# Seven small edits around the rotary keys, the query copies, the first loads and the fillers of a two-block transformer kernel

## The chip, the cores and the metric

The kernel runs on one core of one Trainium2 chip. The metric is the device time of one execution in microseconds; the median of three runs stands for a kernel.

## The reference, cut to what matters

Two transformer blocks are applied one after the other to 512 positions of width 1024. The change touches the input projection and the rotary keys of the first block, the norms after its mixing and after its embedding gate, and the final norm. Of the first block:

```python
u = _rmsnorm(h, g_mix_pre[i])
z = u @ w_in[i]                      # conv 3*512, q_lat 384, kv_lat 256, k_pe 32, gates 2*1024
...
q = (_rmsnorm(q_lat, g_q_lat[i]) @ w_q_up[i]).reshape(bsz, s, N_HEADS, QK_DIM)
kv = (_rmsnorm(kv_lat, g_kv_lat[i]) @ w_kv_up[i])
k_pe = _rope(k_pe[:, :, None, :], positions)      # 32 rotary columns, shared by 8 heads
ob = _chunk_causal_attention(q_full, k_full, v)
...
h = h + _rmsnorm(mixed @ w_o[i], g_mix_post[i])
...
return rmsnorm(h, final_norm)                     # end of the second block
```

The second block reads a memory of 256 positions (`mem`), whose keys and values are also projected.

## The kernel before

**Layout.** Activations lie feature-major: a tile is 128 features by 512 positions. `h` holds the residual stream in 8 tiles. All large products run as three matmuls each (`three`): both operands are split into a high part (type fp32r) and a low part, and high x high, low x high and high x low are added in one PSUM bank of `acc`, which is used as a ring of 4 banks. A tile number `t` uses bank `t % 4`; `open_tile(t)` waits until the tile four before it was taken (`acc_free`, counted in order of tiles by DVE).

**Weights.** They come in units of 128 x 1024 (8 blocks of 128 columns), 333 of them before, in the order in which they are used. SyncE's queue loads unit j into one of 2 raw buffers when the unit two before it has been split (`w_split`); GpSimd (POOL) makes the high and the low part (`split`), in a ring of 4; TensorE (PE) waits for `w_split` at each unit. The first unit is split in two parts (`split_first`: 384 and 640 columns).

**Orders written by hand.** Each engine has one program in order, and they meet by semaphores.

- PE: 12 fillers (`idle`) on a zeroed tile; `spread` (the first three conv tiles side by side, k by k, one k needing one tile of the scaled input); `stationary` and `stationary_loop` (one output tile after another). The order of the input projection is: 12 conv tiles (0 to 11), two small tiles of the distance table (L1243), five latent tiles, one tile of 128 columns with the 32 rotary keys and their turned copy, 16 gate tiles. Then 6 query tiles, 4 value tiles (`moving`), 4 key tiles, 7 tiles of `w_a_out` over the conv output `yhi`, and attention. `memory(layer, sums, roots)` projects the memory over 8 steps k, with the sums of squares of the tile just made (`sum_features`) ahead of step `sums` and their roots spread over the partitions (`spread_roots`) ahead of step `roots`. At the end `again(9)` and `again(2)` stand around the last sums.
- DVE: takes tiles from `acc`; for conv tile group i it takes three tiles, applies the three-tap filter, and writes the low part in `conv_low(i)` after ScalarE (ACT) has written the high part. `conv_low(3)` is the end of the conv part. `times_gain` multiplies a narrow weight by a norm's gain; before the change it is used for `wn` and `wn2`, each followed by `wn_ready`. While it takes key tiles (two of the four), it waits for ACT's copies of the other two (`q_copied`) before it frees their banks.
- ACT: after the gates' sigmoids it waits for `kpe_ready`, copies the rotary keys into the 8 heads of `kf` (8 activations, each waited for), copies four query tiles by `pair`, issues 16 DMAs that place the rotated query halves, and copies two key tiles by `pair`.

`narrow(o, w, width, done)` multiplies a narrow fp32 weight with the raw `h`: k's 8 products go to 128/width strips of output partitions, so with width 32 four of them lie side by side and each strip holds a partial sum.

## Time and profile before

| | |
|---|---|
| median of 3 runs | 2060.71 us (2060.5 to 2061.94) |
| profiled execution, own time | 2061.25 us |
| its span in the trace | 2059.4 us |
| PE busy | 2043.0 us |
| PE weight load busy | 1666.7 us |
| POOL busy | 1274.4 us |
| DVE busy | 974.1 us |
| ACT busy | 576.1 us |

Times in the trace count from the start of the span; L12 is line 12 of the kernel. A PE matmul's duration includes its way through the array, so consecutive matmuls overlap: those of 512 columns start about 0.227 us apart when nothing holds them up, and 24 of them (one output tile over 8 k) take 5.44 us. In a row, "x8" is the number of instructions merged in it, and the bracket gives the idle time of the engine just before it and what ended it.

### The profile page before, as it was taken

To read this page: it belongs to the slowest core of one execution; us is meant where nothing else is said; L and a number is where in the kernel's file an instruction comes from. 1 tells how busy PE (TensorE), PEld (TensorE's weight loads), DVE (VectorE), ACT (ScalarE), POOL (GpSimd) and SP (SyncE) were. 2 spreads that over 40 slices of the span, in tenths; PEclk is the share of its full clock that TensorE was granted. 3 is DMA by queue.
4 is the path that set the end of the run, shared out by engine and by line. 5 is a ranking of instruction groups with operands and counts; after the bars stand their busy time and mean duration, and the time that the engine had idled before them with its cause. 6 is when DMAs were issued, how large, how long until landed. Compare 5 with 4: busy or idle time off the path is not lost.

```text
span 2059.4 us, 29727 instructions
## 1 busy us (share of the span) xinstructions
PE 2043.0 (99%) x10041; PEld 1666.7 (81%) x10041; DVE 974.1 (47%) x1719; ACT 576.1 (28%) x1145; POOL 1274.4 (62%) x846
## 2 busy tenths in 40 slices
PE   9999999999999999999999999999999999999998
PEld 7888768788888887899888888888875588888887
DVE  5452464655552055566455555234367535555311
ACT  3211433422220054323342222000247632222100
POOL 7666638866667668432666666666555566666663
PEclk9999999999999999999999999999999999999999
DMA  5323473323233342221123333334410032332332
GB/s 190 92 92 94 112 106 118 107 92 101 93 107 108 102 148 92 73 62 42 62 92 94 100 93 100 102 106 144 144 42 1 12 102 92 93 101 92 102 107 76
DMA packets 56259, 195.09 MB, mean 95 GB/s; under 512 B 6355, under 2 KB 6803, under 8 KB 55924
## 3 DMA queue, kind: packets, MB, share of 16 engines
q1 hardware_dynamic: 49824, 178.30, 27.7%
q10 hardware_dynamic: 6356, 15.72, 3.4%
q8 instruction: 51, 0.84, 0.2%
q14 instruction: 28, 0.23, 0.0%
HBM read 187.45 MB, written 6.03 MB: 94 GB/s over the span
## 4 chain that ended last, share of the span: by engine, by line
PE 60%; DVE 1%; ACT 1%; issue 0%; DVEq 0%; ACTq 0%
PE acc L859 16%; PE acc L863 16%; PE acc L862 16%; PE acc L1146 2%; PE sc L1163 2%; PE pp L1182 2%; PE acc L1399 1%; PE acc L931 0%; PE pp L1178 0%; DVE s_m L2105 0%; PE acc L1091 0%; PE pp L1377 0%; PE acc L1321 0%; PE pp L1378 0%; PE sc L1377 0%
## 5 line engine op out<-in xcount | busy, mean ns | idle before, releaser
L732 POOL TENSOR_TENSOR wlo<-wraw,whi 128x1024 fp32r<-128x1024 f32 x332 | 801.5, 2414 | 27.7
L730 POOL TENSOR_SCALAR whi<-wraw 128x1024 fp32r<-128x1024 f32 x332 | 351.1, 1057 | 626.6 <-PE acc L859 576.6
L859 PE MATMUL acc<-xhi,whi 128*128 128x512 f32 x1752 | 686.7, 392 | 3.7 <-POOL wlo L744 2.0
L863 PE MATMUL acc<-xlo,whi 128*128 128x512 f32 x1752 | 682.6, 390 | 0.0
L862 PE MATMUL acc<-xhi,wlo 128*128 128x512 f32 x1752 | 682.5, 390 | 0.0
L859 PEld LDWEIGHTS acc<-xhi,whi 128*128 128x128 f32 x1752 | 329.3, 188 | 75.4 <-DVE xlo L1686 5.2
L863 PEld LDWEIGHTS acc<-xlo,whi 128*128 128x128 f32 x1752 | 329.3, 188 | 69.2
L862 PEld LDWEIGHTS acc<-xhi,wlo 128*128 128x128 f32 x1752 | 329.4, 188 | 67.6
L859 PE MATMUL acc<-fhi,whi 128*128 128x512 f32 x528 | 205.4, 389 | 0.0
L862 PE MATMUL acc<-fhi,wlo 128*128 128x512 f32 x528 | 205.4, 389 | 0.0
L863 PE MATMUL acc<-flo,whi 128*128 128x512 f32 x528 | 205.4, 389 | 0.0
L1726 DVE TENSOR_TENSOR u<-acc,rstd 128x512 f32<-128x512 f32 x132 | 91.3, 692 | 203.2 <-PE acc L863 184.5
L2478 ACT ACTIVATE sc<-u,col 128x512 f32<-128x512 f32 x132 | 103.3, 783 | 273.9 <-DVEq L375 272.2
L1696 DVE TENSOR_TENSOR h<-h,acc 128x512 f32<-128x512 f32 x30 | 20.6, 687 | 206.2 <-PE acc L863 206.2
L1736 DVE SCALAR_TENSOR_TENSOR sc<-u,col,sc 128x512 f32<-128x512 f32 x132 | 99.7, 755 | 34.8 <-DVE sc L1737 15.6
L862 PEld LDWEIGHTS acc<-fhi,wlo 128*128 128x128 f32 x528 | 99.1, 188 | 20.7
L859 PEld LDWEIGHTS acc<-fhi,whi 128*128 128x128 f32 x528 | 99.1, 188 | 20.7
L863 PEld LDWEIGHTS acc<-flo,whi 128*128 128x128 f32 x528 | 99.1, 188 | 20.2
L1737 DVE SCALAR_TENSOR_TENSOR sc<-u,col,sc 128x512 f32<-128x512 f32 x132 | 99.7, 755 | 19.4 <-DVE sc L1736 5.1
L2399 ACT ACTIVATE pp<-h 128x512 f32<-128x512 f32 x39 | 23.3, 597 | 270.5 <-DVEq L375 225.0
L2484 ACT ACTIVATE fhi<-pp 128x512 f32 x66 | 39.6, 600 | 146.1 <-DVE pp L1741 146.1
L779 POOL TENSOR_SCALAR s<-s,stat,gt 128x128 f32<-128x128 f32 (+3 forms) x96 | 57.4, 608 | 36.1 <-DVE stat L1770 36.0
(406 smaller groups left out, 2410.2 us busy)
## 6 DMA issues: line engine op xcount, KB each, us to landing
wraw<-in_weights SPq DMA_DIRECT2D x331, 512.0 KB, 3.5
distances<-vr ACTq DMA_DIRECT2D x1, 3840.0 KB
toep<-distances ACTq DMA_DIRECT2D x4, 768.0 KB, 7.6
mem<-in_mem_t ACTq DMA_DIRECT2D x2, 1024.0 KB, 13.9
w<-in_weights ACTq DMA_DIRECT2D x1, 2048.0 KB, 10.7
out_t<-h SPq DMA_DIRECT2D x8, 256.0 KB, 2.4
h<-in_x_t SPq DMA_DIRECT2D x3, 512.0 KB, 7.7
dmf<-in_sums ACTq DMA_DIRECT2D x1, 576.0 KB, 4.3
```

The lines of the kernel that those rows point to most:

```text
L730: nc.gpsimd.tensor_scalar(whi[:, j, :], wraw[:, j % RAW, :], 1.0, 1.0, ALU.mult, ALU.mult).then_inc(sem["w_hi"], 1)
L732: nc.gpsimd.tensor_tensor(wlo[:, j, :], wraw[:, j % RAW, :], plain(whi[:, j, :]), ALU.subtract).then_inc(sem["w_split"], 1)
L779: nc.gpsimd.tensor_scalar(p_, p_, r, c["gate"](j, e) if c["gate"] else 1.0, ALU.mult, ALU.mult).then_inc(sem["pn_ready"], 1)
L859: m = nc.tensor.matmul(o, a_hi, b_hi, start=start, stop=False)
L862: nc.tensor.matmul(o, a_lo, b_hi, start=False, stop=False)
L863: m = nc.tensor.matmul(o, a_hi, b_lo, start=False, stop=stop)
L1146: nc.tensor.matmul(acc[:, plan.bank(c["item"] + 2 * j + e), 0:x["n"]], x["q"][0], x["k"], start=True, stop=True).then_inc(sem["sc_ready"], 1)
L1163: m = nc.tensor.transpose(sc[:, e, b * P:(b + 1) * P], s[:, 2 * c["slot"] + e, a:a + P], ident)
L1726: give(V.tensor_tensor(u[:, half, 2:], src, rstd[:, :], ALU.mult))
L1736: did(V.scalar_tensor_tensor(c, u[:, half, 1:S + 1], w[1], c, ALU.mult, ALU.add))
L1737: n.did(V.scalar_tensor_tensor(c, u[:, half, 0:S], w[0], c, ALU.mult, ALU.add), sem["c_ready"])
L2478: n.did(A.activation(conv[half], u[:, half, 2:], ACT.Identity, scale=w2, bias=b), sem["a_ready"])
```

## The change

Seven edits:

1. **First loads.** Unit 0 is loaded in three pieces (128, 256 and 640 columns), the first two from ACT's queue, the last and unit 1 from SyncE's queue between the tiles of `h`. Units 0, 1 and 2 are split by POOL in 4, 3 and 2 parts (`EARLY`), and PE waits part by part.
2. **Bridge.** 10 fillers instead of 12, then a wait for the first high tile (`hi_ready`), then 3 more.
3. **Rotary keys in column strips.** The unit with the rotary tile is gone (332 units). The 32 columns are loaded as `wk`, multiplied by the gain on DVE after `conv_low(3)` (`wn_ready`, now counted to 3), used by `narrow` right after the two small tiles, scaled into `kraw` on DVE, and four latent tiles later one fp32 matmul with the constant `fold` adds the four strips and makes the turned copy. Two more loads stand in ACT's queue. DVE's product with the cosines and sines now reads this tile, and the sum goes to `kfin`. The gates shift by one tile in the loops.
4. **Query copies first.** On ACT the 8 copies of the rotary keys move from before the query copies to behind the 16 DMA issues.
5. **Norm sums.** `memory(0, 2, 3)` becomes `memory(0, 1, 2)`.
6. **Roots.** `memory(1, 3, 5)` becomes `memory(1, 3, 4)`.
7. **End.** `again(9)` becomes `again(4)`; `again(2)` stays.

```diff
--- before.py
+++ after.py
@@ -48,8 +48,9 @@
 LEVELS = 7
 SW = (1 + 2 + 3 + 4) * P
 LAG = 2
-N_IDLE = 12
-N_AGAIN = 9, 2
+N_IDLE, N_BRIDGE = 10, 3
+EARLY = ((0, 1, 3, 5, 8), (0, 2, 4, 8), (0, 4, 8))
+N_AGAIN = 4, 2
 
 C_TURN = 5
 WIDE = 3
@@ -138,8 +139,7 @@
     at += Q_LORA + KV_LORA
     r = w[:, at:at + ROPE]
     h = ROPE // 2
-    turned = np.concatenate([r[:, h:], r[:, :h]], 1)
-    tiles(np.concatenate([np.zeros((D, NOPE), np.float32), r, turned], 1), [0])
+    rotary = narrow(r, QUAD)
     at += ROPE
     tiles(w, range(at, at + 2 * D, P))
     q = a["w_q_up"][0].reshape(Q_LORA, HA, QK)
...
@@ -295,7 +295,11 @@
 
 
 def fixed():
-    out = np.zeros((P, N_CONST), np.float32)
+
+    out = np.zeros((P, N_CONST + P), np.float32)
+    k, j = np.arange(P)[:, None] % ROPE, np.arange(ROPE)[None, :]
+    out[:, N_CONST + NOPE:N_CONST + QK] = k == j
+    out[:, N_CONST + QK:] = k == (j + ROPE // 2) % ROPE
     out[:, :P] = np.eye(P)
     out[:, P:2 * P] = 1.0
     return out
...
@@ -459,9 +463,13 @@
     va = put("va", [P, TT, HA * VD], 78 * KB)
     cs = put("cs", [P, S], 86 * KB)
     kpe = put("kpe", [P, S], 84 * KB)
+    kfin = put("kfin", [P, S], 32 * KB)
     chunkm = put("chunkm", [P, S], 88 * KB)
     prod = put("prod", [P, S + 2], 78 * KB)
     rstd3 = put("rstd3", [P, S], 78 * KB)
+    wk = put("wk", [P, KD, QUAD], 80 * KB + 256)
+    fold = put("fold", [P, P], 81 * KB + 256)
+    kraw = put("kraw", [P, S], 82 * KB)
     pos_i = nc.alloc_sbuf_tensor_at("pos_i", [P, S], I32, offset=arena + 32 * KB)
     ang = put("ang", [P, 3, S], 34 * KB)
     relv = put("relv", [P, 16], 42 * KB)
@@ -549,7 +557,7 @@
 
         return ap.bitcast(F32)
 
-    names = ("rot_ready rot_placed apart_ready in_first_x in_first_w in_soon in_wn in_wn2 wn_ready lr_raw w_open w_first w_split out_ready out_done w_used w_hi acc_free x_ready acc_ready ss_added rs_ready rt_ready rq_ready rs_taken "
+    names = ("in_wk in_fold kraw_ready rot_ready rot_placed apart_ready in_first_x in_first_w in_second_w part_hi part_split in_soon in_wn in_wn2 wn_ready lr_raw w_open w_split out_ready out_done w_used w_hi acc_free x_ready acc_ready ss_added rs_ready rt_ready rq_ready rs_taken "
              "o_free bc_ready sc_ready pn_ready act_copied dve_copied t_ready pv_done r_ready sc_clear kc_ready qn_ready cs_scored cp_ready cr_ready cn_ready ct_ready pc_ready mq_ready zw_ready in_w1 mm_ready x_free prod_ready tap_ready y_ready yh_ready mix_ready mh_ready in_rel in_bk in_const "
              "qkv_ready lr_ready in_wg in_sums la_ready e_ready g_ready kout_ready st_ready og_ready "
              "hid_ready gln_ready in_toep dve_step sq_ready src_ready u_ready c_ready a_ready v_ready "
@@ -695,9 +703,12 @@
 
         sp.dma_start(h[:, 0, :], x_t[:, 0, :]).then_inc(sem["in_first_x"], 16)
         sp.dma_start(h[:, 1, :], x_t[:, 1, :]).then_inc(in_x[0], 16)
-        for j in range(1, 4):
+        sp.dma_start(wraw[:, 0, EARLY[0][2] * P:UNIT], weights[0, :, EARLY[0][2] * P:UNIT]).then_inc(loaded[0], 16)
+        sp.dma_start(h[:, 2:4, :], x_t[:, 2:4, :]).then_inc(in_x[1], 16)
+        load(1, 1)
+        for j in range(2, 4):
             sp.dma_start(h[:, 2 * j:2 * j + 2, :], x_t[:, 2 * j:2 * j + 2, :]).then_inc(in_x[j], 16)
-        sp.dma_start(const[:, :], consts).then_inc(sem["in_const"], 16)
+        sp.dma_start(const[:, :], consts[:, 0:N_CONST]).then_inc(sem["in_const"], 16)
         sp.dma_start(col[:, N_SOON:], cols[:, N_SOON:]).then_inc(sem["in_col"], 16)
         for j in range(RAW, RING):
             sp.wait_ge(sem["w_split"], j - RAW + 1)
@@ -732,17 +743,23 @@
             nc.gpsimd.tensor_tensor(wlo[:, j, :], wraw[:, j % RAW, :], plain(whi[:, j, :]),
                                     ALU.subtract).then_inc(sem["w_split"], 1)
 
-        def split_first():
-
+        def split_early(unit):
+
+            parts = list(zip(EARLY[unit], EARLY[unit][1:]))
+            before = sum(len(x) - 2 for x in EARLY[:unit])
             pool.sem_inc(sem["w_open"], 1)
-            for part, done, come in ((slice(0, WIDE * P), "w_first", sem["in_first_w"]),
-                                     (slice(WIDE * P, UNIT), "w_split", loaded[0])):
-                pool.wait_ge(come, 16)
-                nc.gpsimd.tensor_scalar(whi[:, 0, part], wraw[:, 0, part], 1.0, 1.0, ALU.mult, ALU.mult)\
-                    .then_inc(sem["w_hi"] if done == "w_split" else sem["w_first"], 1)
-                pool.wait_ge(sem["w_hi"] if done == "w_split" else sem["w_first"], 1)
-                nc.gpsimd.tensor_tensor(wlo[:, 0, part], wraw[:, 0, part], plain(whi[:, 0, part]),
-                                        ALU.subtract).then_inc(sem[done], 1)
+            for i, (first, last) in enumerate(parts):
+                if unit == 0 and i < 2:
+                    pool.wait_ge(sem[("in_first_w", "in_second_w")[i]], 16)
+                else:
+                    pool.wait_ge(loaded[unit], 16)
+                part, ends = slice(first * P, last * P), i == len(parts) - 1
+                high = sem["w_hi"] if ends else sem["part_hi"]
+                nc.gpsimd.tensor_scalar(whi[:, unit, part], wraw[:, unit % RAW, part], 1.0, 1.0, ALU.mult, ALU.mult)\
+                    .then_inc(high, 1)
+                pool.wait_ge(high, unit + 1 if ends else before + i + 1)
+                nc.gpsimd.tensor_tensor(wlo[:, unit, part], wraw[:, unit % RAW, part], plain(whi[:, unit, part]),
+                                        ALU.subtract).then_inc(sem["w_split" if ends else "part_split"], 1)
 
         def splits(first, last):
             at = first
@@ -786,8 +803,9 @@
             r = cst[:, j, 2, :].unsqueeze(2).to_broadcast([P, 16, 32])
             nc.gpsimd.tensor_tensor(p_, p_, r, ALU.mult).then_inc(sem["cn_ready"], 1)
 
-        split_first()
-        splits(1, U_LATENT + RING - 1)
+        for unit in range(len(EARLY)):
+            split_early(unit)
+        splits(len(EARLY), U_LATENT + RING - 1)
         normalise(plan_a, s_a)
         splits(U_LATENT + RING - 1, U_UP0 + WIDE)
         add_squares(SQ_UP0, 0, KD // 2)
@@ -884,9 +902,12 @@
                     if turn == 0 and m >= apart:
                         open_tile(t + m - apart)
                     piece = turn * WIDE + m
-                    if un == 0 and piece == 0:
-                        pe.wait_ge(sem["w_first"], 2)
-                    elif piece % 8 == 0 or (un == 0 and piece == WIDE):
+                    if un < len(EARLY):
+                        if piece % 8 in EARLY[un][:-2]:
+                            pe.wait_ge(sem["part_split"], sum(len(x) - 2 for x in EARLY[:un]) + EARLY[un].index(piece % 8) + 1)
+                        elif piece % 8 == EARLY[un][-2]:
+                            pe.wait_ge(sem["w_split"], un + 1)
+                    elif piece % 8 == 0:
                         pe.wait_ge(sem["w_split"], un + 1)
                     slot, c = un % RING, piece % 8 * P
                     three(sc[:, m, :] if m < apart else bank(t + m - apart), whi[:, slot, c:c + P], wlo[:, slot, c:c + P], x_hi[:, k, :],
@@ -1230,6 +1251,8 @@
 
 
         idle(N_IDLE)
+        pe.wait_ge(sem["hi_ready"], 1)
+        idle(N_BRIDGE)
         spread(xhi, xlo)
         pe.wait_ge(sem["in_const"], 16)
         xs += KD
@@ -1244,10 +1267,21 @@
                              start=True, stop=True).then_inc(sem["acc_ready"], 1)
             t += 1
 
-        stationary_loop(xhi, xlo, 2)
+        pe.wait_ge(sem["wn_ready"], 1)
+        open_tile(t)
+        narrow(bank(t), wk, QUAD, sem["acc_ready"])
+        t += 1
+        stationary_loop(xhi, xlo, 1)
+        pe.wait_ge(sem["kraw_ready"], 1)
+        pe.wait_ge(sem["in_fold"], 16)
+        open_tile(t)
+        nc.tensor.matmul(bank(t), fold[:, :], kraw[:, :], start=True, stop=True).then_inc(sem["acc_ready"], 1)
+        t += 1
+        stationary_loop(xhi, xlo, 1)
         stationary(xhi, xlo, KD, 2, between={(0, 2): lambda: sum_features(3), (0, 6): lambda: spread_roots(root_t),
                                              (1, 2): lambda: sum_features(2), (1, 6): lambda: spread_roots(root_t)})
-        stationary_loop(xhi, xlo, 3)
+        stationary_loop(xhi, xlo, 2)
+        stationary(xhi, xlo, KD, 3)
         xs += KC_
 
         mark["q"] = t
@@ -1270,7 +1304,7 @@
         stationary(xhi, xlo, KD, KD, fresh=KD, between={(3, 0): lambda: sum_features(KD, MEM // P),
                                                         (3, 3): lambda: spread_roots(rstd_mt, MEM // P)})
         xs += KD
-        memory(0, 2, 3)
+        memory(0, 1, 2)
         mark["up0"] = feed_forward(False)
         mark["down0"] = t
         pe.wait_ge(sem["x_ready"], xs + 2)
@@ -1282,11 +1316,11 @@
         stationary(xhi, xlo, KD, 5)
 
 
-        memory(1, 3, 5)
+        memory(1, 3, 4)
         spread(xhi, xlo)
         xs += KD
         def low_rank():
-            pe.wait_ge(sem["wn_ready"], 1)
+            pe.wait_ge(sem["wn_ready"], 2)
             narrow(sc[:, 0, :], wn, QUAD, sem["lr_raw"])
             spread_roots(rstd_t)
 
...
@@ -1840,6 +1874,11 @@
         dve.wait_ge(sem["rs_ready"], rs)
         did(V.tensor_copy(rstd[:, :], pv))
         n.did(V.tensor_tensor(rstd2[:, :], pv, rstd[:, :], ALU.mult), sem["rs_taken"])
+        def times_gain(w, gain, name):
+            dve.wait_ge(sem[name], 16)
+            n.did(V.tensor_tensor(w[:, :, :], w[:, :, :], C(gain, 0, KD).unsqueeze(2).to_broadcast([P, KD, w.shape[-1]]),
+                                  ALU.mult), sem["wn_ready"], False)
+
         dve.wait_ge(sem["in_col"], 16)
 
         def angles():
@@ -1886,20 +1925,22 @@
             if i == 1:
                 angles()
         conv_low(KC_ - 1)
+        times_gain(wk, "mix_pre", "in_wk")
 
         for n0, n1 in ((0, S), (S, TW)):
             give(V.tensor_copy(vr[0:NH, n0:n1], take(NH, n1 - n0)))
         n.tell(sem["vr_ready"])
+        give(V.tensor_tensor(kraw[:, :], take(), rstd[:, :], ALU.mult))
+        n.tell(sem["kraw_ready"])
 
         dve.wait_ge(sem["sine_ready"], 1)
         did(V.tensor_scalar(cs[r, :], cs[r, :], C("sign", p=r), None, ALU.mult))
         n.tell(sem["cs_ready"])
         for i in range(5):
+            if i == 4:
+                give(V.tensor_tensor(kpe[r, :], take()[r, :], cs[r, :], ALU.mult))
             give(V.tensor_tensor(lat[:, i, :], take(), rstd[:, :], ALU.mult))
             n.tell(sem["src_ready"])
-
-        give(V.tensor_tensor(kpe[r, :], take()[r, :], rstd[r, :], ALU.mult))
-        did(V.tensor_tensor(kpe[r, :], kpe[r, :], cs[r, :], ALU.mult))
 
         def gate(i):
             give(V.tensor_tensor(sg[:, i, :], take(), rstd[:, :], ALU.mult))
...
@@ -2018,11 +2059,6 @@
         add_square(False, of=sqbanks)
         stage_after(e, "ple_post", "nmix0", meanwhile={1: lambda: memory_out(1)})
 
-
-        def times_gain(w, gain, name):
-            dve.wait_ge(sem[name], 16)
-            n.did(V.tensor_tensor(w[:, :, :], w[:, :, :], C(gain, 0, KD).unsqueeze(2).to_broadcast([P, KD, w.shape[-1]]),
-                                  ALU.mult), sem["wn_ready"], False)
 
         times_gain(wn, "nmix0", "in_wn")
         invert(rstd_t)
@@ -2531,11 +2567,8 @@
             return [x[:, k, :] for k in range(count)]
 
         load(col[:, 0:N_SOON], cols[:, 0:N_SOON], "in_soon")
-        soon = WIDE * P
-        load(wraw[:, 0, 0:soon], weights[0, :, 0:soon], "in_first_w")
-        act.dma_start(wraw[:, 0, soon:UNIT], weights[0, :, soon:UNIT]).then_inc(loaded[0], 16)
-        for j in range(1, RAW):
-            act.dma_start(wraw[:, j, :], weights[j]).then_inc(loaded[j], 16)
+        for first, last, name in zip(EARLY[0], EARLY[0][1:], ("in_first_w", "in_second_w")):
+            load(wraw[:, 0, first * P:last * P], weights[0, :, first * P:last * P], name)
         act.wait_ge(sem["in_soon"], 16)
         warm(ACT.Sqrt)
         for k in range(KD):
@@ -2555,6 +2588,8 @@
                 load(row[:, :], rws, "in_row")
                 load(pos_i[NOPE:P, :], positions, "in_pos")
                 load(chunkm[:, :], chunk, "in_chunk")
+                load(wk[:, :, :].rearrange("p a b -> p (a b)"), weights[N_UNITS + 4, :, UNIT - KD * QUAD:UNIT], "in_wk")
+                load(fold[:, :], consts[:, N_CONST:N_CONST + P], "in_fold")
             if i == 1:
                 act.wait_ge(sem["angle_ready"], 1)
                 n.did(A.activation(cs[NOPE:P, :], ang[NOPE:P, 0, :], ACT.Sin), sem["sine_ready"])
@@ -2574,9 +2609,6 @@
             act.wait_ge(sem["gate_in"], i + 1)
             n.did(A.activation(sg[:, i, :], sg[:, i, :], ACT.Sigmoid), sem["sig_ready"])
 
-        act.wait_ge(sem["kpe_ready"], 1)
-        for i in range(HA):
-            did(A.activation(kf[NOPE:QK, i, :], kpe[NOPE:QK, :], ACT.Copy, scale=-QK ** -0.5))
         def pair(to, tile, first, scale):
 
             act.wait_ge(sem["acc_ready"], tile + 1)
@@ -2592,6 +2624,9 @@
             for hd in range(HA):
                 at = NOPE + (hd + side) % 2 * half
                 act.dma_start(qf[at:at + half, hd, :], sq[hd * half:(hd + 1) * half, side, :]).then_inc(sem["rot_placed"], 16)
+        act.wait_ge(sem["kpe_ready"], 1)
+        for i in range(HA):
+            did(A.activation(kf[NOPE:QK, i, :], kfin[NOPE:QK, :], ACT.Copy, scale=-QK ** -0.5))
         for i in range(1, 4, 2):
             pair(kf, mark["k"] + i, 2 * i, -QK ** -0.5)
         act.wait_ge(sem["q_copied"], HA // 2 + 2)
```

## Rows read from the trace of the kernel before

**Rows 1.** The page's first part: busy time, share of the span and instructions, by engine.
```profile
PE 2043.0 (99%) x10041; PEld 1666.7 (81%) x10041; DVE 974.1 (47%) x1719; ACT 576.1 (28%) x1145; POOL 1274.4 (62%) x846
```

**Rows 2.** Waits of PE over the whole span: total us, times, longest.
```profile
PE acc L859 <- POOL wlo L744: 2.0, 1, 2.0
PE acc L859 <- DVE xlo L1686: 1.8, 2, 1.0
```

**Rows 3.** Windows: length, then busy us of PE, PEld, DVE, ACT, POOL; PEclk, DMA, GB/s.
```profile
7.55:10.85 3.30, 3.30 (x8) 2.57 (x9) 2.58 (x4) 3.23 (x7) 2.33 (x3) 0.50 1.02 413
10.95:13.00 2.05, 2.05 (x11) 1.68 (x10) 1.46 (x3) 2.02 (x4) 1.97 (x2) 1.00 1.04 374
2052.00:2055.00 3.00, 0.00 (x0) 0.00 (x0) 3.00 (x6) 0.60 (x1) 2.24 (x2) 1.00 0.57 223
2057.00:2059.00 2.00, 0.00 (x0) 0.00 (x0) 0.00 (x0) 0.00 (x0) 0.00 (x0) 0.50 0.80 305
```

**Rows 4.** Timeline of the start: start us, duration us, engine, line, operation.
```profile
1.07 4.37 PE L842 MATMUL acc<-tmp 128*128 128x128 f32 x24 [1.07 <-DVE tmp L1572]
...
5.91 0.69 DVE L1646 TENSOR_TENSOR xlo<-sc,xhi 128x512 fp32r<-128x512 f32 x1 [4.90 <-ACT xhi L2416]
6.28 0.99 POOL L744 TENSOR_TENSOR wlo<-wraw,whi 128x384 fp32r<-128x384 f32 x1
...
7.42 0.68 PE L859 MATMUL acc<-xhi,whi 128*128 128x512 f32 x1 [1.98 <-POOL wlo L744]
```

**Rows 5.** Timeline of PE and DVE at the end of the conv tiles, and `times_gain` on `wn`.
```profile
75.97 1.24 PE L1243 MATMUL acc<-bk,relv 33*12 33x512 f32 x4
...
79.95 0.69 DVE L1872 TENSOR_TENSOR ylo<-sc,yhi 128x512 fp32r<-128x512 f32 x1 [0.80 <-ACT yhi L2551]
...
88.39 0.69 DVE L1898 TENSOR_TENSOR lat<-acc,rstd 128x512 f32<-128x512 f32 x1 [4.75 <-PE acc L863]
...
810.56 0.42 DVE L2024 TENSOR_TENSOR wn<-wn,col 128x256 f32<-128x256 f32 x1
```

**Rows 6.** Timeline of PE: fp32 products, `narrow` with width 32 and one of 512 columns.
```profile
817.07 1.92 PE L999 MATMUL sc<-h,wn 128*32 128x512 f32 x16
...
247.82 1.02 PE L1146 MATMUL acc<-kf,qf 96*128 96x512 f32 x2
```

**Rows 7.** Timeline of ACT and its queue from the rotary keys' copies to the key copies.
```profile
204.72 5.26 ACT L2579 ACTIVATE kf<-kpe 32x512 f32<-32x512 f32 x8 [3.19 <-DVEq L375]
...
214.85 8.14 ACTq L2594 DMA_DIRECT2D qf<-sq  x12
223.04 2.45 ACT L2584 ACTIVATE kf<-acc 64x512 f32<-64x512 f32 x4 [8.12 <-PE acc L863]
```

**Rows 8.** Timeline of PE: first value, first key and second `w_a_out` tile.
```profile
212.09 0.39 PE L859 MATMUL acc<-whi,lathi 128*128 128x512 f32 x1
...
218.58 0.39 PE L859 MATMUL acc<-lathi,whi 128*128 128x512 f32 x1
...
226.74 0.39 PE L859 MATMUL acc<-yhi,whi 128*128 128x512 f32 x1
```

**Rows 9.** Timeline of PE (step k = 1 of the first `memory`) and of DVE.
```profile
351.67 0.28 PE L859 MATMUL acc<-mem0hi,whi 128*128 128x256 f32 x1
...
351.91 0.69 DVE L1612 TENSOR_TENSOR sqsum<-sqsum,pp 128x512 f32<-128x512 f32 x1 [0.77 <-ACT pp L2399]
...
362.25 0.88 DVE L1826 TENSOR_TENSOR mkt<-acc,rstd_m 128x256 f32<-128x256 f32 x2 [2.56 <-PE acc L863]
```

**Rows 10.** Timeline of DVE behind its take of the second `memory`'s tiles.
```profile
796.03 0.76 DVE L1676 SCALAR_TENSOR_TENSOR sc<-e,col,pp 128x512 f32<-128x512 f32 x1 [0.54 <-DVEq L375]
```

**Rows 11.** Timeline of the end: fillers, ACT's two scaled tiles and its root.
```profile
2046.45 2.20 PE L848 MATMUL acc<-fhi 128*128 128x512 f32 x9
...
2048.20 1.33 ACT L2806 ACTIVATE h<-h,col 128x512 f32<-128x512 f32 x2
...
2050.37 0.26 ACT L2463 ACTIVATE root_t<-pp,col 128x4 f32<-128x4 f32 x1 [0.83 <-PE pp L1037]
```

More of the change, by code:

```diff
@@ L193, in weight_units @@
         tiles(a["cmp_w1_2"][j], [0])
-    u.extend(_pack(few))
+    u.extend(_pack(few + rotary))
     return np.stack(u)
@@ L338 @@
 U_FFN_UP, U_FFN_DOWN = 2 * KF_, 3 * KD
-N_UNITS = (34 + 3 + 2 + 4 + 4 + 8 + U_FFN_UP + U_FFN_DOWN + 2 + 8
+N_UNITS = (33 + 3 + 2 + 4 + 4 + 8 + U_FFN_UP + U_FFN_DOWN + 2 + 8
            + 4 + 8 + 12 + 8 + U_FFN_UP + U_FFN_DOWN
            + 8 + 4 + 4 + 8 + 8 + U_FFN_UP + U_FFN_DOWN)
-U_LATENT = 34 + 3 + 2 + 4
+U_LATENT = 33 + 3 + 2 + 4
 N_SQUARES = 93
@@ L1518, in _ @@
             hidden(j)
-        pe.wait_ge(sem["wn_ready"], 2)
+        pe.wait_ge(sem["wn_ready"], 3)
         open_tile(t)
@@ L1915, in _ @@
             add_square(k == 0)
-        for i in range(2):
+        for i in range(3):
             gate(i)
@@ L1920, in _ @@
             add_square(k == 0)
-        gate(2)
+        gate(3)
         latent(0)
         invert()
-        gate(3)
+        gate(4)
         factor(rstd3[:, :])
@@ L1927, in _ @@
             latent(i)
-            gate(3 + i)
-        for i in range(8, 16):
+            gate(4 + i)
+        for i in range(9, 16):
             gate(i)
@@ L1932, in _ @@
         did(V.tensor_copy(tmp[rot, :], kpe[swapped, :]))
-        did(V.tensor_tensor(kpe[rot, :], kpe[rot, :], tmp[rot, :], ALU.add))
+        did(V.tensor_tensor(kfin[rot, :], kpe[rot, :], tmp[rot, :], ALU.add))
         n.tell(sem["kpe_ready"])
```

## The prediction

> **What bounds the kernel now.** I began with the page: PE is busy for 2043.0 of 2059.4 us [rows 1], so the span is PE's own work plus 16.4 us, of which 7.4 us lie behind its last matmul. A change can only help by taking matmuls away, by closing one of PE's pauses, or by shortening the two ends; it harms wherever it makes PE wait. PE's waits, the second view, are few: 2.0 us for the first split weights and 1.8 us in two places for a low part of the input [rows 2]. The third view is the windows of the start: PE's granted clock is 0.50, the level of 1.2 GHz, from about 7.5 to 10.9 us, and 1.00 (2.4 GHz) after [rows 3]. The fillers end at 5.44, the first real matmul starts at 7.42 [rows 4], and the clock falls just behind it. Eight matmuls run in these 3.4 us that would take half of it: 1.6 us lost. At the end the clock is still 1.00 up to 3.0 us after PE's last matmul, and 0.50 from 5.0 us after it [rows 3]. So I expect PE's clock to fall around a pause of 4 us, which is longer than the 2.0 us before the one fall and the 3.0 us over which the end still shows 1.00. The last views are timelines of the places that the change touches.
>
> I sum against the profiled execution's own 2061.25 us; it lies 0.54 above the median of 2060.71, and I take that off at the end.
>
> **First loads and bridge: -2.35.** PE's start at 7.42 waits for POOL's low part of 384 columns (6.28 + 0.99); the other operand is ready at 5.91 + 0.69 = 6.60 [rows 4]. The first part now has 128 columns, a third of the bytes and of the POOL work, which takes more than the needed 0.7 us out of POOL's chain. PE then starts on the other operand at about 6.67: -0.75. The reordered loads move the same bytes: the DMA engines carry 413 GB/s in this stretch [rows 3], so the 0.33 MB of unit 0 that now stand ahead of h's third and fourth tile delay these by 0.8 us at most, at a place where ACT works through the tiles one by one and is not waiting for a load. POOL has more and smaller instructions; should one of its parts come late, PE waits some tenths (bound +0.5), and I count 0. Ten fillers end at about 5.0 (two of the fast ones fewer); the bridge can start behind the first high part, whose end starts DVE at 5.91 [rows 4], and its 3 fillers take 0.6 us. PE's longest pause is then 1.0 instead of 2.0 us. I take the clock to hold: -1.6. If it does not, this term is 0; no row shows a pause pattern like this one, so both ends stay.
>
> **Rotary keys: +1.5, and +1.6 of clock.** Gone is one output tile, 24 matmuls: DVE takes such tiles 4.75 + 0.69 = 5.44 us apart [rows 5]. In its place stand `narrow` with width 32, 1.92 us, and one fp32 matmul of 512 columns, 1.02 us (the nearest row has 96 contracted partitions instead of 128, the same two passes) [rows 6]. That alone would be -2.5. But `narrow` now waits for the gain, and DVE puts it there only after `conv_low(3)`. The two small tiles end at 75.97 + 1.24 = 77.2; the last conv low part ends at 79.95 + 0.69 = 80.64, the gain on 256 columns takes 0.42 [rows 5], so PE can go on at about 81.2. What is queued behind the wait is everything: PE has one order, and the latent tiles stand behind `narrow`. Pause: +4.0. It cannot be filled by DVE being earlier, as DVE's chain (filter taps, ACT's high part, low part) starts with the last conv tile, which PE makes just ahead of the small tiles. The sum of this edit is -2.5 + 4.0 = +1.5. The second wait, for `kraw`, has four tiles (21.8 us) of cover, and ACT's two additional loads are issued some 40 us ahead: both 0. The pause is longer than the one after which the clock fell, so I add what that fall cost, 1.6 (bounds 0 and 1.7, half of the 3.4 us) [rows 3].
>
> The Trainium skill (TensorE: Matmul & The Clock Gate, "Measured speedup vs the span model") gives three column strips a speedup of 2.38, which carried on to four would be 3.2. The eight products here take 1.92 us in strips; one after another, at up to 1.02 each, they would be 7 to 8 us, a factor of about 4, so the trace is better than the page [rows 6]. By that rule `narrow` would be an estimated 2.2 to 2.6 us and the sum 0.3 to 0.7 higher; I stay with the row.
>
> **Query copies first: +2.9, and +1.6 of clock.** What it gains: the 8 value steps take 218.58 - 212.09 = 6.49 us where 8 x 0.68 = 5.44 would do, since the banks of the last query tiles come free late [rows 8]. With the copies ahead of the rotary ones that is gone: -1.05. What it costs: ACT's issue of the 16 DMAs starts when the last query tile is there, before and after, and ends at 214.85 + 8.14 = 222.99; the key copies start right behind, at 223.04 [rows 7], though their first tile was ready at 221.3 (two key tiles of 1.36 us each behind 218.58). Into this place now come the 8 rotary copies of 5.26 us in all [rows 7]. The first key pair is then copied at 228.3 + 1.2 = 229.5. Behind it wait DVE (it frees the bank only then) and, through the ring of four banks, the second `w_a_out` tile on PE. That tile starts at 226.74 [rows 8]; it would be due at 225.7 with the value steps' gain, and can start at 229.65. Net +2.9, with a pause of 4.0 us. The later tiles have their banks in time. Again the clock: +1.6, bounds 0 and 1.7.
>
> **Norm sums: +1.0.** In the first `memory` the sums move one step ahead, to the start of step 1 at 351.67; the last square is added only at 351.91 + 0.69 = 352.60 [rows 9]. PE waits 1.0. The earlier roots buy nothing: DVE has two tiles to spare and then waits for `memory`'s own tiles until 362.25 [rows 9], which now come 1.0 later, and PE's wait behind it stays. In the second `memory` the roots come one step (1.4 us) earlier, but DVE's next step at 796.03 waits for ACT's copy of the last `memory` tiles [rows 10]: 0 (bounds -0.8, the wait in rows 2, and 0).
>
> **End: -0.8.** Nine fillers take 2.20 us, 0.22 apart; five fewer are -1.1. ACT's root waited 0.83 us for the sums; without that it is held by its own two scaled tiles, which end at 2049.53 [rows 11]. So -0.8 of the 1.1 arrive, and the output behind shifts with it.
>
> **Sum.** -2.35 + 1.5 + 1.6 + 2.9 + 1.6 + 1.0 - 0.8 = +5.45, or 2066.7 for an execution like the profiled one, and 2066.2 us beside the median.
>
> **The rivals.**
>
> *The clock does not fall in the pauses.* Then both 1.6 are gone: +2.25, 2063.0; one of two, 2064.6. For it: the end's clock held for 3.0 us; against: 4.0 is longer than that. Chance 0.2.
>
> *The bridge does not keep the clock.* The 1.6 of the first term stay lost: +7.05, 2067.8. For it: the fall at 7.5 came 2.1 us after the fillers, and PE still rests for 1.0 us. Chance 0.2.
>
> *Not slower, the rotary copies are covered.* If the 16 issues do not hold ACT up as read (they start before the last query tile, or the copies run under them), the key copies are done in time, and the place costs nothing: 5.45 - 3.96 - 1.6 = -0.1, 2060.6. It decides when the first key pair is copied before 225.7. Against it: the issues and the copy behind them abut to 0.05 us. Chance 0.08.
>
> *The gain is there in time.* Without the pause at `narrow`: 5.45 - 4.0 - 1.6 = -0.15, 2060.5; it decides when `wn_ready` comes before 77.2. DVE's order speaks against it. Chance 0.07. Both covers together would be faster, 2054.9: included there with 0.03.
>
> **How the numbers follow.** My forecast has 0.45: its own range, with clock losses of 0.8 to 1.7 each and 0.3 for each pause, is 2064.6 to 2067.2. What a measurement can tell from no change is 0.2%, 4.1 us, so the border lies at 2064.8. Slower: nearly all of 0.45, all of 0.2 for the bridge, little of the unfallen clock: 0.63. Faster: 0.05. Within: 0.32. The range goes from 2062.4, the unfallen clock with a little room, to 2068.4, the failed bridge with room; outside it are the two covers.
>
> **What would show it.** PE: first real matmul near 6.7 and clock 1.00 through 7 to 11 us; an idle time of 4 us at `narrow`, ended by DVE's gain on `wk`; one of 4 us at the second `w_a_out` tile, ended by ACT's key copy; 1 us at the first `memory`'s sums; clock 0.50 for up to 3.4 us behind the two long ones; ACT's last root without idle time. The prediction is wrong if PE's order has no gap at one of the two long places, or if the clock behaves otherwise in two of the three.

## The result, and the profile after

The changed kernel takes 2067.98 us, the median of 7 executions (2067.08 to 2070.78); the kernel before, in the same comparison, 2061.45 us (7 executions, 2060.5 to 2062.69). The ratio is 1.0034, with a 95% interval of 1.0025 to 1.0043: slower by 6.5 us. The forecast was slower, 2066.2, with a range of 2062.4 to 2068.4. The time lies in the range but above the likeliest case's own (2064.6 to 2067.2), 1.8 us over the forecast; 0.74 of that is in the kernel before, whose median was 0.74 higher in this comparison than in the runs that the forecast was set beside.

The profiled execution took 2067.98 us with a span of 2066.2. From its page, the engines' busy time, as in [rows 1]:

```profile
PE 2043.0 (99%) x10032; PEld 1663.2 (80%) x10032; DVE 976.2 (47%) x1720; ACT 576.1 (28%) x1145; POOL 1274.3 (62%) x854
```

PE's busy time is the same to 0.1 us, though an output tile of 24 matmuls has gone: what the tile gave has been taken back by matmuls that ran at half the clock. PE's waits over the whole span, as in [rows 2]:

```profile
PE acc L1020 <- DVE wk L1879: 3.9, 1, 3.9
PE acc L877 <- DVEq L379: 3.3, 1, 3.3
PE acc L877 <- DVE xlo L1720: 1.9, 2, 1.0
...
PE pp L1053 <- issue: 0.9, 1, 0.9
PE acc L877 <- POOL wlo L761: 0.7, 1, 0.7
PE acc L860 <- ACT xhi L2452: 0.5, 1, 0.5
```

The 2.0 us for the first weights are replaced by 0.5 (ahead of the bridge) and 0.7 (for the second part of unit 0), and two long waits stand above everything else. The start, on PE and then on POOL, beside [rows 4]:

```profile
1.06 4.22 PE L860 MATMUL acc<-tmp 128*128 128x128 f32 x20 [1.06 <-DVE tmp L1606]
5.80 0.94 PE L860 MATMUL acc<-tmp 128*128 128x128 f32 x6 [0.52 <-ACT xhi L2452]
6.53 0.50 PE L877 MATMUL acc<-xhi,whi 128*128 128x512 f32 x1
...
8.19 0.50 PE L877 MATMUL acc<-xhi,whi 128*128 128x512 f32 x1 [0.70 <-POOL wlo L761]
```

```profile
5.62 0.46 POOL L761 TENSOR_TENSOR wlo<-wraw,whi 128x128 fp32r<-128x128 f32 x1
6.92 0.41 POOL L758 TENSOR_SCALAR whi<-wraw 128x256 fp32r<-128x256 f32 x1 [0.84 <-DMA wraw<-in_weights]
7.41 0.72 POOL L761 TENSOR_TENSOR wlo<-wraw,whi 128x256 fp32r<-128x256 f32 x1
```

The first real matmul is at 6.53 instead of 7.42. The second step could follow at 7.32, 0.23 us behind the matmul at 7.09, and starts at 8.19, because POOL waited for its second load. The place of `narrow`, on PE and then on DVE, beside [rows 5, 6]:

```profile
74.61 1.24 PE L1266 MATMUL acc<-bk,relv 33*12 33x512 f32 x4
79.80 3.59 PE L1020 MATMUL acc<-h,wk 128*32 128x512 f32 x16 [3.94 <-DVE wk L1879]
83.32 0.50 PE L877 MATMUL acc<-xhi,whi 128*128 128x512 f32 x1
```

```profile
78.59 0.69 DVE L1911 TENSOR_TENSOR ylo<-sc,yhi 128x512 fp32r<-128x512 f32 x1 [0.79 <-ACT yhi L2584]
79.32 0.42 DVE L1879 TENSOR_TENSOR wk<-wk,col 128x256 f32<-128x256 f32 x1
```

DVE makes the last low part, then the gain, and PE goes on when the gain is done. `narrow` takes 3.59 us where [rows 6] has 1.92 for as many matmuls. The key copies, on ACT and its queue, then on PE, beside [rows 7, 8]:

```profile
214.54 9.57 ACTq L2626 DMA_DIRECT2D qf<-sq  x15
224.16 5.24 ACT L2629 ACTIVATE kf<-kfin 32x512 f32<-32x512 f32 x8 [9.04 <-issue]
229.43 2.44 ACT L2616 ACTIVATE kf<-acc 64x512 f32<-64x512 f32 x4
```

```profile
213.70 0.39 PE L877 MATMUL acc<-whi,lathi 128*128 128x512 f32 x1
...
219.14 0.39 PE L877 MATMUL acc<-lathi,whi 128*128 128x512 f32 x1
...
227.07 0.39 PE L881 MATMUL acc<-ylo,whi 128*128 128x512 f32 x1
230.74 0.79 PE L877 MATMUL acc<-yhi,whi 128*128 128x512 f32 x1 [3.27 <-DVEq L379]
```

The copies stand in one chain: issues, rotary copies, key pair at 229.43 + 1.2, and PE at 230.74. The eight value steps take 5.44 us, as forecast. The windows with the granted clock in the third column from the end, beside [rows 3]:

```profile
7.00:11.00 4.00, 3.30 (x15) 2.25 (x14) 2.66 (x4) 3.73 (x7) 3.75 (x7) 1.00 1.02 410
79.95:83.30 3.35, 3.35 (x16) 0.44 (x12) 0.66 (x2) 0.00 (x0) 0.00 (x0) 0.51 0.00 0
228.00:230.00 2.00, 0.00 (x0) 0.00 (x0) 0.00 (x0) 1.91 (x4) 0.68 (x1) 1.00 0.17 10
230.00:236.80 6.80, 6.06 (x14) 4.78 (x15) 2.50 (x4) 3.29 (x6) 0.00 (x0) 0.50 0.20 74
```

The fall at the start is gone. There is one of 3.4 us at `narrow` and one of 6.8 us at the second `w_a_out` tile. (At the very end the clock falls too, as in the kernel before; here it does so behind PE's last matmul.) The first `memory` and the end, beside [rows 9, 11]:

```profile
358.42 0.28 PE L881 MATMUL acc<-wlo,mem0hi 128*128 128x256 f32 x1
359.56 1.02 PE L1053 MATMUL pp<-const,sqsum 128*128 128x1 f32 x8 [0.86 <-issue]
```

```profile
2054.18 1.07 PE L866 MATMUL acc<-fhi 128*128 128x512 f32 x4
...
2055.93 1.34 ACT L2841 ACTIVATE h<-h,col 128x512 f32<-128x512 f32 x2
...
2057.17 0.24 ACT L2499 ACTIVATE root_t<-pp,col 128x4 f32<-128x4 f32 x1
```

PE stops for 0.86 us ahead of the sums, and ACT's root follows its two scaled tiles without idle time. Two small differences lie in and behind the first block's attention, and nobody forecast them. The first is in the trace before, where PE once sat idle for 0.86 us; none of the other 13 traces has that. The second is in the trace after, where PE waits for a split unit:

```profile
272.93 0.27 PE L1182 MATMUL pp<-pt_a,va 128*64 128x128 f32 x1 [0.86 <-issue]
```

```profile
318.15 0.47 PE L877 MATMUL acc<-xhi,whi 128*128 128x512 f32 x1 [0.27 <-POOL wlo L743]
```

Nine of the ten traces with the rotary keys in strips have this wait, and none of the four without them, so it goes with that edit; why the unit comes later there isn't shown. Laid out along PE's order, the difference between the two traces is this. Each measured entry is the growth of the shift between two places that both traces have (the small tiles 75.97 to 74.61, the first latent tile 77.14 to 83.32, the first value step 212.09 to 213.70, behind the second fall 239.66 to 246.62, in attention 275.76 to 282.08, and so on); a pause and the clock behind it are parted by the due time of the matmul.

| term | forecast | measured |
|---|---|---|
| start: earlier matmul, clock kept, late part | -2.35 | -1.36 |
| pause at `narrow` | +4.0 | +3.95 |
| `narrow` itself | +1.92 | +1.92 |
| tile gone, `fold` in its place | -4.42 | -4.57 |
| clock behind `narrow`'s pause | +1.6 | +1.67 |
| value steps without their stalls | -1.05 | -1.05 |
| key copies late | +3.96 | +3.44 |
| clock behind that pause | +1.6 | +2.96 |
| idle time in attention that only the trace before has | 0 | -0.64 |
| split unit late behind attention, and rest | 0 | +0.55 |
| norm sums | +1.0 | +0.86 |
| end | -0.8 | -0.93 |
| sum | +5.46 | +6.80 |

### The profile page after: what moved, and what is told of

It is laid out like the page before. It is cut to its first block, busy times and chain, and to the rows that moved or that the text cites. A ratio compares the mean times of both kernels' runs of the same rounds, so it can differ in the third digit from the quotient of the medians.

```text
span 2066.2 us, 29709 instructions
## 1 busy us (share of the span) xinstructions
PE 2043.0 (99%) x10032; PEld 1663.2 (80%) x10032; DVE 976.2 (47%) x1720; ACT 576.1 (28%) x1145; POOL 1274.3 (62%) x854
## 4 chain that ended last, share of the span: by engine, by line
PE 59%; DVE 1%; ACT 1%; issue 0%; DVEq 0%; ACTq 0%
PE acc L877 16%; PE acc L880 16%; PE acc L881 16%; PE acc L1167 2%; PE sc L1184 2%; PE pp L1203 2%; PE acc L1433 1%; PE acc L952 0%; PE pp L1199 0%; DVE s_m L2141 0%; PE acc L1112 0%; PE pp L1411 0%; PE acc L1355 0%; PE pp L1412 0%; PE sc L1411 0%
```

## The experiments

Each was timed against the kernel before on the same chip. Medians of runs a few us apart are told with their range, since executions of one kernel differ here by 1 to 7 us.

### One part undone at a time, then all three

**The gain ahead of its wait.** In the changed kernel, the gain moves from behind `conv_low(3)` into the loop over the conv groups:

```diff
+            if i == 2:
+                times_gain(wk, "mix_pre", "in_wk")
         conv_low(KC_ - 1)
-        times_gain(wk, "mix_pre", "in_wk")
```

> The changed kernel, with one line of DVE's order moved: the gain goes on wk after the third conv group instead of the fourth. Theory (the pause at narrow is DVE's order, 3.9 us, and the clock's fall behind it costs 1.7): both go, -5.6 us against the changed kernel (2067.98), about 2062.4; PE shows no wait at narrow, narrow takes 1.9 instead of 3.6 us, the clock stays 1.00. Rival 1 (the clock fell for another reason, such as the fp32 strips themselves): only -3.9, narrow still 3.6 us. Rival 2 (PE waits there for something else behind the gain, such as the bank): under 1 us gained.

Measured: 2061.03 us (2059.11 to 2064.5, 11 runs) against 2061.61; ratio 1.0000 [0.9992, 1.0009]. That is 6.5 above before turned into 0.6 below, 7.1 us for one line. PE at the place:

```profile
74.49 1.24 PE L1266 MATMUL acc<-bk,relv 33*12 33x512 f32 x4
75.67 1.93 PE L1020 MATMUL acc<-h,wk 128*32 128x512 f32 x16
```

The pause is gone and `narrow` takes 1.93 us, at full clock. The place is worth pause and clock together, 3.95 + 1.67 in the trace. Of the rest, 1.3 us come from the other clock fall, which in this trace is 3.4 us long (225.6 to 229.0) and not 6.8: behind it PE is 7.04 us ahead of the changed kernel, 0.12 of that from the start. That part isn't the moved line's as far as is shown, since the length of the fall also differs between other kernels. The wait at the `w_a_out` tile stays at 3.3 us, so the two pauses are separate.

**Key pairs ahead of the rotary copies.**

```diff
+        for i in range(1, 4, 2):
+            pair(kf, mark["k"] + i, 2 * i, -QK ** -0.5)
         act.wait_ge(sem["kpe_ready"], 1)
         ...
-        for i in range(1, 4, 2):
-            pair(kf, mark["k"] + i, 2 * i, -QK ** -0.5)
```

> The changed kernel, with ACT's eight rotary copies moved once more, behind the two pairs of key copies. Theory (these copies, behind the 16 DMA issues, hold back the key copies by 5.2 us, PE rests 3.5 us at the second w_a_out tile and then runs 6 us at half clock, 2.9 us lost): -6.4 us against the changed kernel, about 2061.6; the rotary copies end some 10 us ahead of attention. Rival (the DMA issues alone hold the key copies, so the order behind them is not what counts): under 1 us gained.

Measured: 2063.95 us (2060.92 to 2068.17, 11 runs); ratio 1.0011 [1.0003, 1.0020]. By the medians -4.0 against the changed kernel; the profiled execution has 2061.42, -6.6. ACT in it:

```profile
224.60 2.46 ACT L2616 ACTIVATE kf<-acc 64x512 f32<-64x512 f32 x4 [9.04 <-PE acc L881]
227.08 5.25 ACT L2631 ACTIVATE kf<-kfin 32x512 f32<-32x512 f32 x8
```

The key copies start behind the issues, PE does not wait at the `w_a_out` tile at all, and nobody needs the rotary copies before they are done. The pause is caused by the order of the copies, not by the issues alone. The 11 executions spread widely, four below 2062, five from 2062.8 to 2064.5 and two near 2068, and the profiled one is the second fastest; what differs in the others isn't in any trace. So 4.0 is the figure for the median, and 6.6 that of one fast execution.

**Norm sums back** (`memory(0, 1, 2)` to `memory(0, 2, 3)`).

> The changed kernel with memory(0, 2, 3) again. Theory (PE waits 0.86 us for the last square, and the earlier roots buy nothing): -0.9 us, about 2067.1. Rival (the earlier roots do shorten the wait behind memory, and hide in it): 0 to +1.0.

Measured: 2067.66 us (7 executions from 2066.09 to 2069.85, and one of 11728.84, which nothing explains); ratio 1.0029 [1.0018, 1.0039]. PE's wait ahead of the sums is gone, the profiled execution is 1.9 us shorter than that of the changed kernel, but the medians differ by only 0.3. This run doesn't show the 0.9: in its trace the clock falls elsewhere too, before and not after `narrow` starts, and for twice as long (the one at the `w_a_out` tile is 3.4 us long, from 231.4 to 234.8, half of that in the changed kernel):

```profile
77.60:84.50 6.90, 5.17 (x20) 1.91 (x21) 3.29 (x6) 0.42 (x1) 0.62 (x1) 0.51 0.00 0
```

A term below 1 us is smaller than what the falls of the clock differ by between these two traces, so this run can't settle it.

**All three together** on the changed kernel.

> The changed kernel with all three edits (gain early, key pairs ahead of the rotary copies, sums back). Theory (the three prices add up, nothing else is late next): -5.6 - 6.4 - 0.9 = -12.9 us against the changed kernel, about 2055.1, that is 6.4 below the kernel before. Rival (a wait behind them is uncovered, in the gates or in attention): above 2058.

Measured: 2054.76 us (2054.22 to 2058.54, 8 runs) against 2061.61, ratio 0.9972 [0.9961, 0.9982]: 6.85 us faster than the kernel before, and 13.2 faster than the change as made (12.9 were expected). The earlier roots of the second `memory` (edit 6) stay in it. PE's longest waits:

```profile
PE acc L877 <- DVE xlo L1720: 1.9, 2, 1.0
PE acc L1509 <- DVE o_g L2239: 1.1, 2, 0.8
```

These are waits that the kernel before has as well. The clock is 1.00 up to 2044.5; from there to the end of the span it is 0.50, and the last of PE's eight products with the roots run in that stretch: the eight take 1.44 us, where they take 1.09 in the changed kernel.

### The clock, apart from the pause

**Fillers in both long pauses.** The waits stay; PE works through matmuls that nobody reads, 16 ahead of `narrow` and 15 ahead of the second `w_a_out` tile, into `ptp`:

```diff
+        def keep_busy(x, count):
+            for _ in range(count):
+                nc.tensor.matmul(ptp[:, :], x[:, 0, 0:P], x[:, 1, :], start=True, stop=True)
...
+                if m == 1 and busy:
+                    keep_busy(yhi, busy)
...
+        keep_busy(xhi, 16)
```

> The changed kernel, with 16 and 15 fp32r fillers of 512 columns put into PE's two pauses (ahead of narrow's wait, and ahead of the wait of the second w_a_out tile); their results are used by nobody. The waits themselves stay. Theory (besides the pauses, PE loses 1.3 to 3.4 us behind each, only because its clock has fallen): the clock stays at 1.00, narrow takes 1.9 us, the two places cost 3.9 and 3.5 us and no more; -4.0 to -5.0 against the changed kernel (2067.98), about 2063.5. Rival (the slow matmuls behind the pauses have another cause, such as late operands): no gain, or +0.3 for fillers that are too long.

Measured: 2064.69 us (2062.96 to 2065.91, 11 runs) against 2061.51; ratio 1.0014 [1.0005, 1.0023], 3.3 us below the changed kernel. PE at the two places, then the windows behind them:

```profile
76.25 3.96 PE L871 MATMUL pp<-xhi 128*128 128x512 f32 x16
80.27 1.92 PE L1027 MATMUL acc<-h,wk 128*32 128x512 f32 x16
...
226.13 3.56 PE L871 MATMUL pp<-yhi 128*128 128x512 f32 x15
229.58 0.50 PE L882 MATMUL acc<-yhi,whi 128*128 128x512 f32 x1
```

```profile
80.00:86.00 6.00, 5.95 (x34) 3.60 (x34) 2.80 (x5) 1.66 (x3) 3.10 (x2) 1.00 0.00 0
230.00:236.00 6.00, 6.00 (x28) 4.94 (x27) 2.90 (x5) 2.18 (x4) 2.88 (x2) 1.00 0.07 27
```

`narrow` starts as late as before but takes 1.92 us, and both windows are at 1.00. So the clock is a cost of its own that follows an idle PE, and it was 3.3 us here by the medians, 4.1 between the two profiled executions (2063.88 against 2067.98, though PE waits 0.5 us longer for POOL at the start of this one), against 1.67 + 2.96 = 4.6 in the changed kernel's trace and 3.2 in the forecast.

### The start

**No bridge.** The changed kernel with `N_IDLE, N_BRIDGE = 12, 0` instead of `10, 3`.

> The changed kernel, with 12 fillers ahead and none behind the first high part. Theory (the three fillers of the bridge keep the clock): the clock falls at the start in most executions as in the kernel before, +1.0 to +1.7 us, about 2069.3. Rival (the earlier first matmul alone keeps it): unchanged within 0.4.

Measured: 2067.61 us (2067.16 to 2069.37, 8 runs) against 2061.51; ratio 1.0029 [1.0019, 1.0040], nothing that differs from the change as made. PE, and the clock behind:

```profile
1.06 4.50 PE L860 MATMUL acc<-tmp 128*128 128x128 f32 x24 [1.06 <-DVE tmp L1606]
6.72 0.47 PE L877 MATMUL acc<-xhi,whi 128*128 128x512 f32 x1 [1.16 <-DVE xlo L1680]
```

```profile
7.00:11.00 4.00, 3.71 (x16) 2.64 (x15) 2.77 (x4) 3.93 (x7) 3.75 (x7) 1.00 1.01 404
```

PE rests for 1.16 us and the clock holds, where it fell behind the 1.98 us of [rows 2]. The bridge is not needed for that.

**One load for the first 384 columns**, with POOL's parts as in the change:

```diff
-        for first, last, name in zip(EARLY[0], EARLY[0][1:], ("in_first_w", "in_second_w")):
-            load(wraw[:, 0, first * P:last * P], weights[0, :, first * P:last * P], name)
+        load(wraw[:, 0, 0:EARLY[0][2] * P], weights[0, :, 0:EARLY[0][2] * P], "in_first_w")
```

> The changed kernel, with the first 384 columns loaded by one DMA, as before the change, but still split by POOL in two parts. Theory (the second load of 256 columns landed at 6.85 us where the single one of 384 had landed at 5.64, and PE's 0.7 us wait for the second part comes from that): the first matmul starts near 6.8 instead of 6.53, the second wait shrinks to 0.4 or less; -0.2 to -0.6 us. Rival (POOL's pace sets the second part, not the load): 0 or +0.3.

Measured: 2068.42 us (2066.9 to 2070.07, 6 runs); ratio 1.0033 [1.0020, 1.0045]. That is no gain where 0.2 to 0.6 us were expected. The wait for the second part is gone, but POOL starts at 6.09 instead of 5.23, and PE pays that at once:

```profile
6.19 1.65 PE L860 MATMUL acc<-tmp 128*128 128x128 f32 x6 [0.49 <-ACT xhi L2452]
7.49 0.77 PE L877 MATMUL acc<-xhi,whi 128*128 128x512 f32 x1
8.07 0.63 PE L880 MATMUL acc<-xhi,wlo 128*128 128x512 f32 x1
```

The matmuls stand 0.43 us apart up to 10.2, as at the lower level, and the six fillers ahead of them took 1.65 us instead of 0.94, although the clock's column says 1.00 there. The small tiles start at 75.74, 1.1 later than in the changed kernel. Why this start ran slowly stays open.

**The new start alone**, on the kernel before (loads, `split_early`, bridge).

> The kernel before, with the first loads and the bridge alone. The changed kernel's trace says that this place gave 1.36 us (first matmul 0.9 earlier, clock held 1.6, second part waited for 0.9, the rest in slightly slower matmuls). Theory 1 (the fall of the clock in the kernel before is the rule): -1.0 to -1.6 us, near 2060.2. Theory 2 (the clock falls at the start only in some executions of the kernel before, so that the bridge saves little in the median): -0.5 to +0.2.

Measured: 2059.28 us (2058.84 to 2059.9, 11 runs) against 2061.6; ratio 0.9987 [0.9978, 0.9997]: -2.3, the forecast's -2.35 and not the -1.36 of the trace of the whole. In its trace the wait for the second part is 0.33 us, and the small tiles start 1.62 us earlier than in the trace before (74.35 against 75.97). Another 0.6 lie in attention, where only the trace before has its idle time. If that belongs to most executions of the kernel before, the start is worth 1.7 and not 2.3; the medians can't part the two.

**The old start in the mended kernel** (the loads and 12 fillers of before; the roots of the second `memory` go back to step 5 too, whose effect no run shows by itself).

> The mended kernel (strips with the gain early, query copies, key pairs, rotary copies; sums and roots where they were; again(4)) with the loads and 12 fillers of the kernel before. Sum of the parts: -2.6 -1.05 -0.9 = -4.5 to -5.0 against the kernel before, near 2056.8, 1 to 2 us above the mended kernel (2054.76). Rival (the new start is worth nothing in the median): within 0.5 of the mended kernel.

Measured: 2057.04 us (2055.78 to 2058.71, 11 runs); ratio 0.9977 [0.9968, 0.9986], 2.3 above the mended kernel. PE's pause is 1.89 us, and the clock is 0.50 from 8.5 to 12.0; the small tiles start 2.27 us later (76.37 against 74.10). By the medians both directions give 2.3 us. The end of this trace is slower as well, by 0.5 us, since the clock falls at 2046.2, ahead of PE's last eight products:

```profile
2046.23 1.97 PE L1053 MATMUL pp<-const,root_t 128*128 128x128 f32 x8 [0.17 <-DVE root_t L1639]
```

### The other parts alone, on the kernel before

**Query copies first**, with `kfin` for the rotary keys so that their copies can come later.

> The kernel before, with the order of ACT's copies alone (rotary copies behind the 16 DMA issues; the summed rotary keys are written to a tile of their own so that nothing overwrites them). Theory: the value steps lose their 1.05 us of waits, PE rests about 3.5 us at the second w_a_out tile and runs at half clock for 3 to 6 us behind it; +2.4 + 1.7 to 3.0 = +4.1 to +5.4 against the kernel before, near 2066. Rival (the edit only hurts in the company of the strips): at most +1.

Measured: 2066.42 us (2065.8 to 2067.57, 10 runs) against 2061.51; ratio 1.0023 [1.0013, 1.0033], +4.9. In its trace PE waits 4.1 us at the second `w_a_out` tile, and the clock is 0.50 from 228.5 to 235.3. This trace also tells something of the start, which is that of the kernel before. PE's first pause was only 1.01 us and the clock held, but then PE waited for the rest of unit 0:

```profile
11.09 0.47 PE L860 MATMUL acc<-xhi,whi 128*128 128x512 f32 x1 [1.19 <-POOL wlo L745]
```

The small tiles start at 76.26, no earlier than the 75.97 of the trace before, where the clock fell.

**The end alone** (`N_AGAIN` from `9, 2` to `4, 2`).

> The kernel before, with again(4) in place of again(9). Theory (ACT's root waited 0.83 us for the sums): -0.8 to -0.9 us. Rival (the shorter run of fillers lets something else come late): 0.

Measured: 2060.59 us (2059.9 to 2060.96, 11 runs) against 2061.6; ratio 0.9993 [0.9984, 1.0002], -1.0.

**The strips with the gain in time** (the rotary keys' edit, with the gain behind the third conv group).

> The kernel before, with the rotary strips alone and the gain put on wk after the third conv group. Theory (24 matmuls of 5.44 us in all give way to 1.9 and 0.87 us, with no wait): -2.6 us, near 2058.9. Rival (the two additional loads or the shifted gate tiles cost something): above 2060.

Measured: 2058.77 us (2057.68 to 2061.65, 11 runs); ratio 0.9987 [0.9978, 0.9996], -2.8. Its trace shows the same at the start: the clock held behind a pause of 1.43 us, PE waited 0.82 us for unit 0 later, and the small tiles start at 75.88.

Added up: start -2.3, end -1.0, strips -2.8, query copies +4.9, the late gain +7.1 (the changed kernel less the one with the gain early), norm sums +0.5 (by the medians less certain than the others: 1.0029 against 1.0034) give +6.4; the whole change measures +6.5. The agreement is closer than the parts are known: each carries some tenths, the late gain's 7.1 hold 1.3 of the other clock fall, the four differences against the kernel before can each hold the 0.6 us that its trace has in attention, and edit 6 was never timed alone.

## Where the forecast held, and which steps failed

The direction and the places were right, and the change of +6.5 against +5.5 is near. Two terms of the sum failed. The clock behind the key copies' pause, "again the clock: +1.6, bounds 0 and 1.7", measured 2.96, outside its bounds. And at the first loads, "should one of its parts come late, PE waits some tenths (bound +0.5), and I count 0" measured 0.87.

**The views and what bounds the kernel.** Right. All that cost or gave more than 0.7 us happened in PE's order, at the places named, with the releasers named.

**First loads and bridge, -2.35.** Right alone (-2.3 twice), 1 us too good in the profiled execution of the whole. The step that counted 0 for a late part failed there: the second part's load landed at about 6.85 and PE lost 0.87. PE's idle time there is 0.70 in this trace, 0.3 with the start alone and without the bridge, 1.2 with the fillers, 1.5 with the key pairs first, and nothing in two others, so it is a spread and not a fixed price. The mechanism given for the 1.6 us isn't shown. The clock holds without the bridge too, so the bridge isn't what keeps it. And with the loads of before it also held in two of five traces, in which PE then waited for unit 0 instead and the small tiles came no earlier. What the traces do show is the sum: the small tiles start at 75.9 to 76.4 in the five traces with the old start and at 74.1 to 75.3 in eight of the nine with new loads (75.74 with one load). That the total of -2.35 came out so well is in part luck.

**Rotary keys, +1.5 and +1.6.** Right in each term: pause 3.95 for 4.0, `narrow` 1.92, clock 1.67 for 1.6. For `fold` 1.02 was taken from 96 partitions, and its own row has 1.02 too; but the next matmul starts before it ends, and its place in PE's order takes 0.87. The forecast did not have the wait for a split unit behind attention, 0.27 us. The strips themselves are good: -2.8 where the gain is in time, forecast -2.5. The Trainium skill's factor for column strips (TensorE: Matmul & The Clock Gate, "Measured speedup vs the span model") would have made `narrow` an estimated 2.2 to 2.6 us; 1.92 and 1.93 at full clock decide for the row.

**Query copies, +2.9 and +1.6.** The mechanism was right, and its gain exact (1.05). The 16 issues took 10.2 us in this trace and ended 0.5 earlier against the value steps than [rows 7] made them, so the pause was 3.44 for 3.96. The clock term is the one that was mis-sized. Its upper bound came from a single fall of 3.4 us. This one was 6.8 us long, with PE busy for 6.06 of them: 2.96 us lost. With the query order alone it was 6.8 us again; with the gain early, 3.4.

**Norm sums, +1.0.** 0.86 in the trace, 0.3 to 0.5 by the medians, which can't resolve it. That the earlier roots buy nothing fits the traces, in which no step was found that got faster; no run has them alone.

**End, -0.8.** -0.93, and -1.0 alone. ACT's root is held by its own tiles, as forecast. What the forecast did not have: in three of the ten traces with `again(4)` (one load, mended, old start) the clock falls before PE's last eight products are done, which then take 1.44 to 1.97 us instead of 1.09 and cost up to 0.5 us. In the four traces with `again(9)` it falls behind them. Whether the five fillers make that difference isn't shown.

**Together.** Against the forecast's +5.46 the trace has +1.0 at the start, +1.36 in the second clock fall, -0.5 in the copies and -0.5 in the small terms: +6.80. The two surprises around attention (-0.64 and +0.55) nearly cancel, which is luck. Two sums of the forecast were a little off: its own range, with two clock losses of 0.8 to 1.7 and 0.3 for each of two pauses, would be 2064.0 to 2067.0 and not 2064.6 to 2067.2, and both covers together 2055.0 and not 2054.9; the measured time lies outside the first in either form. The rival "the clock does not fall in the pauses" did not come true: the clock fell at both, in every trace that had them unfilled. Neither did the two covers, but each is one small move away: that is what the early gain and the early key pairs did.

## What to carry to other kernels

An operation put ahead of a wait is only as early as the last thing that its producer does before it: look up the producer's place in its own engine's order, with every DMA issue that stands there (0.64 us each on ACT here), and move the producer first. Price a pause of the engine that bounds the kernel as the pause and the clock behind it, here 1.7 to 3.0 us more, and take the upper bound of that from the longest low stretch that any run shows, not from one. Time the parts of a bundle alone before judging it: start, end and strips were worth -6 us together, and two producers that stood one place too late in their engines' orders turned the whole into +6.5.
